# Experts sorted by token count on chip: four of eight in 64 slots with two products, weight splits in pairs, gates at the slots

## The reference

```python
logits = (t @ w_router).astype(jnp.float32)
top_vals, top_idx = lax.top_k(logits, TOP_K)
top_w = jax.nn.softmax(top_vals, axis=-1)
gates = jnp.sum(jax.nn.one_hot(top_idx, N_EXPERTS, dtype=jnp.float32) * top_w[..., None], axis=1)
out = jnp.zeros_like(t)
for e in range(N_EXPERTS):
    out = out + gates[:, e:e + 1].astype(t.dtype) * swiglu(t, w_gate[e], w_up[e], w_down[e])
```

## Time and profile before

| | |
|---|---|
| median of 3 runs | 1240.27 us |
| profiled execution, its own time | 1239.24 us |
| its span in the trace | 1237.4 us |
| mean granted TensorE clock | 0.993 of full |
| busy share: TensorE, weight loads, VectorE, ScalarE | 98%, 83%, 74%, 65% |
| bytes moved, mean rate | 294.48 MB, 238 GB/s |

### The profile page before, as it was taken

The page is one execution under the profiler, slowest core; times in us unless marked ns, Lnnn a source line. Parts: engine busy times, 40 slices in busy tenths (PEclk is TensorE's granted clock), DMA queues, the critical chain, the costliest instruction groups (busy, mean ns, idle before and its releaser), DMA issues.

```text
span 1237.4 us, 16333 instructions
## 1 busy us (share of the span) xinstructions
PE 1210.3 (98%) x5945; PEld 1029.4 (83%) x5945; DVE 920.6 (74%) x1157; ACT 802.2 (65%) x1035; POOL 17.9 (1%) x59
## 2 busy tenths in 40 slices
PE   8999999999999999999999999999999999999995
PEld 7887788888888888877888898888888888888884
DVE  5567666765545464686667699999989998999995
ACT  6555566454343455465564588888787888888882
POOL 2000000000000000000000000000000000000000
PEclk9999999999999999999999999999999999999997
DMA  9745423586555255554236489999999999999980
GB/s 325 231 144 184 137 93 111 181 294 231 185 177 196 94 162 199 162 170 162 90 111 203 169 306 382 331 347 352 338 341 332 358 340 344 332 354 347 362 306 36
DMA packets 119868, 294.48 MB, mean 238 GB/s; under 512 B 8958, under 2 KB 33628, under 8 KB 119276
## 3 DMA queue, kind: packets, MB, share of 16 engines
q1 hardware_dynamic: 118832, 288.66, 67.4%
q0 software_dynamic: 816, 4.75, 1.0%
q10 hardware_dynamic: 140, 0.04, 0.0%
HBM read 292.37 MB, written 1.05 MB: 237 GB/s over the span
## 4 chain that ended last, share of the span: by engine, by line
PE 90%; ACT 3%; DVE 3%; issue 2%; DMA 1%; SPq 0%; DVEq 0%; POOLq 0%; POOL 0%; ACTq 0%
PE bank L1316 27%; PE bank L1318 27%; PE bank L1317 27%; PE bank L1354 2%; DMA raw<-in_w_in 1%; PE bank L1638 1%; ACT w_hi L564 1%; PE bank L1661 1%; PE bank L1515 1%; PE bank L1495 1%; ACT p_buf L687 1%; DVE mixed L1065 1%; PE bank L1503 1%; PE bank L1487 1%; PE bank L1655 1%
## 5 line engine op out<-in xcount | busy, mean ns | idle before, releaser
L874 DVE TENSOR_TENSOR w_lo<-raw,w_hi 128x1536 fp32r<-128x1536 f32 (+3 forms) x144 | 242.9, 1693 | 178.6 <-ACT w_hi L564 178.0
L1316 PE MATMUL bank<-w_hi,aT_hi 128*128 128x512 f32 (+2 forms) x848 | 330.9, 390 | 3.4 <-DVE aT_lo L905 2.8
L1318 PE MATMUL bank<-w_hi,aT_lo 128*128 128x512 f32 (+2 forms) x848 | 324.3, 382 | 0.0
L1317 PE MATMUL bank<-w_lo,aT_hi 128*128 128x512 f32 (+2 forms) x848 | 324.0, 382 | 0.0
L1145 DVE SCALAR_TENSOR_TENSOR w_lo<-raw,cols,w_hi 128x896 fp32r<-128x896 f32 x256 | 287.7, 1150 | 32.7 <-ACT w_hi L740 29.0
L564 ACT ACTIVATE w_hi<-raw 128x1536 fp32r<-128x1536 f32 (+4 forms) x144 | 205.7, 1433 | 159.1 <-PE bank L1318 157.6
L740 ACT ACTIVATE w_hi<-raw,cols 128x896 fp32r<-128x896 f32 x256 | 265.5, 1045 | 64.9 <-PE bank L1318 61.6
L1316 PEld LDWEIGHTS bank<-w_hi,aT_hi 128*128 128x128 f32 x848 | 159.8, 188 | 29.9 <-DVE w_lo L970 2.1
L1318 PEld LDWEIGHTS bank<-w_hi,aT_lo 128*128 128x128 f32 x848 | 159.7, 188 | 26.7
L1317 PEld LDWEIGHTS bank<-w_lo,aT_hi 128*128 128x128 f32 x848 | 160.0, 189 | 24.5
L1316 PE MATMUL bank<-w_hi,bT_hi 128*128 128x448 f32 (+1 forms) x384 | 146.9, 382 | 0.7 <-issue 0.7
(11 more groups left out here) (230 smaller groups left out, 1119.6 us busy)
## 6 DMA issues: line engine op xcount, KB each, us to landing
raw<-in_moe_w_gate SPq DMA_DIRECT2D x128, 448.0 KB, 4.7
raw<-in_moe_w_up SPq DMA_DIRECT2D x128, 448.0 KB, 4.8
raw<-in_moe_w_down SPq DMA_DIRECT2D x112, 512.0 KB, 5.6
raw<-in_w_in SPq DMA_DIRECT2D x40, 768.0 KB, 4.5
raw<-in_dense_w_gate SPq DMA_DIRECT2D x22, 512.0 KB, 4.0
raw<-in_dense_w_up SPq DMA_DIRECT2D x22, 512.0 KB, 4.8
raw<-in_dense_w_down SPq DMA_DIRECT2D x11, 1024.0 KB, 4.9
raw<-in_w_in SPq DMA_DIRECT2D x20, 512.0 KB, 4.7
```

What stands on the lines that cost most here:

```text
L874: dve.tensor_tensor(w_lo[:, s, 0:n], raw[:, b % 2, j, 0:n], w_hi[:, s, 0:n].bitcast(F32), ALU.subtract).then_inc(lo_made[j], 1)
L1316: pe.matmul(dst, x_hi, b_hi, start=start, stop=False)
L1317: pe.matmul(dst, x_hi, b_lo, start=False, stop=False)
L1318: return pe.matmul(dst, x_lo, b_hi, start=False, stop=stop)
```

## The change

1. **Sorting.** The tokens per expert are counted as before; a key per expert (8 times the count, less its number; 4096 more for expert 0) is sorted by MAX, and `rank_of` reorders the slot numbers and gates by two multiplications and a reduction (`by_rank`). `order` holds the experts' numbers; SP reads one with `value_load` before each expert from the second on and loads its weights from the address it gives. Ranks 0 to 3 are the big experts of the four pairs, ranks 4 to 7 the small ones, as (big, small) pairs.
2. **64 slots, two products.** A small expert's stationary operand holds 64 tokens' high parts in its columns 0 to 63 and the low parts of the same tokens in 64 to 127; `small_product` multiplies both by w_hi and by w_lo. The low rows are then added to the high rows: ScalarE copies the bank (`fold_low`), TensorE adds it shifted by 64 rows (`add_folded`), once for the gate and once for the up product of a step. For the down product no folding is made: the rows of `sel` transposed stand twice, so `bring_back` adds both. The hidden of a small expert has 64 rows, is transposed in one go and evacuated by one instruction on each engine. A second round now also runs if the fifth key says more than 64 tokens.
3. **Paired splits.** Two neighbouring granules of one width in an even place are split by one instruction (`SPLITS`); raw slots and split slots come free by pairs.
4. **Gates at the slots.** `gates_to_slots` brings each slot's gate to its row, y_hi and y_lo are scaled by it (`slot_gate`), and one `bring_back` sums both experts of a pair, so `add_output` is a plain addition, 16 times instead of 32.
5. **Channel weights on the residual.** `weigh` makes hg = h * gain before routing; the splits have no scale. The gain buffer is loaded with `norm_ffn[1]`, then again with `norm_final` by the POOL queue.
6. `BETWEEN` is written anew for this.

```diff
+def is_small(k):
+    return k % 4 >= 2
+SPLITS = []
+for i in range(0, len(GRANULES), 2):
+    SPLITS += [(i, 2)] if granule_width(GRANULES[i][2]) == granule_width(GRANULES[i + 1][2]) else [(i, 1), (i + 1, 1)]
...
+BETWEEN = {(STEPS - 1, 22): ("hidden", STEPS - 1, 0)}
+for p in range(PAIRS_E):
+    k = 4 * p
+    BETWEEN[k, 11], BETWEEN[k, 13] = ("gate", p, 0), ("sel", p, 0)
+    for q, n in enumerate((3, 9)):
+        BETWEEN[k + 1, n], BETWEEN[k + 2, n] = ("hidden", k, q), ("hidden", k + 1, q)
+    BETWEEN[k + 3, 5] = ("hidden", k + 2, 0)
+    if p:
+        BETWEEN[k, 5] = ("hidden", k - 1, 0)
+        for q, n in enumerate((1, 5, 7, 11)):
+            BETWEEN[k + 2, n] = ("back", p - 1, q)
+    if p < PAIRS_E - 1:
+        for i, at in enumerate(((2, 13), (2, 15), (3, 1), (3, 3), (3, 7), (3, 9), (3, 11), (3, 13))):
+            BETWEEN[k + at[0], at[1]] = (("tokens_hi", "tokens_lo")[i // 4], p + 1, i % 4)
...
+                                    experts_at[k // 2] = sp.value_load(order[0:1, at_rank:at_rank + 1], min_val=0, max_val=EXPERTS - 1)
-                                sp.wait_ge(e_lo_made, RAW_BEFORE[i] + 1)
+                                sp.wait_ge(e_lo_made, SPLIT_OF[RAW_BEFORE[i]] + 1)
...
+                    if W_BEFORE[i] is None:
+                        act.wait_ge(used[i // 2], MIX[1] + BLK_MIX + 2)
+                    else:
+                        act.wait_ge(e_used, W_BEFORE[i + n - 1] + 1)
+                    act.activation(split_of(hi_slot, m), raw_of(i, n), ACT.Copy).then_inc(e_hi_made, 1)
...
+            def fold_low(r, k, banks, part):
+                s = small_steps(r, k)
+                act.wait_ge(e_used, SEQ[r, k, (KC, GU_N)[part] - 1] + 1)
+                if 2 * s + part:
+                    act.wait_ge(e_folded, 2 * s + part)
+                for u in range(2):
+                    act.activation(fold[:, u * HN:(u + 1) * HN], bank[banks[u]][:, 0:HN], ACT.Copy).then_inc(e_fold_made, 1)
...
+                def weigh(u):
+                    for t in range(NT):
+                        wait_read(dve, L, PAIR_MIX + u, t)
+                        part = slice(u * NB, (u + 1) * NB)
+                        dve.tensor_tensor(hg[:, t, part], h[:, t, part], gain[:, part], ALU.mult).then_inc(weighed, 1)
...
-                    dve.scalar_tensor_tensor(out=w_of(lo_slot, i), in0=raw_of(i), scalar=granule_scale(i),
-                                             in1=w_of(hi_slot, i).bitcast(F32), op0=ALU.mult, op1=ALU.subtract).then_inc(e_lo_made, 1)
+                    dve.tensor_tensor(split_of(lo_slot, m), raw_of(i, n), split_of(hi_slot, m).bitcast(F32),
+                                      ALU.subtract).then_inc(e_lo_made, 1)
...
+            def small_product(dst, x, b_hi, b_lo, start, stop):
+                pe.matmul(dst, x, b_hi, start=start, stop=False)
+                return pe.matmul(dst, x, b_lo, start=False, stop=stop)
+            def add_folded(r, k, banks, part):
+                s = small_steps(r, k)
+                for u in range(2):
+                    pe.wait_ge(e_fold_made, 4 * s + 2 * part + u + 1)
+                    last = pe.matmul(bank[banks[u]][:, 0:HN], shift[:, :], fold[:, u * HN:(u + 1) * HN], start=False, stop=True, skip_group_check=True)
+                last.then_inc(e_folded, 1)
```

382 lines of the change are left out of this document (250 added, 132 removed).

## The result

| | before | changed |
|---|---|---|
| median | 1239.53 us (4 runs) | 1211.74 us (4 runs, 1211.41 to 1212.18) |
| ratio, 95% interval | | 0.977 (0.976 to 0.978) |
| profiled execution | 1239.24 us | 1211.82 us |

What follows compares the result with a forecast made beforehand. TensorE was taken to bound the stage before, three engines nearly level after. Stage -29.7, ahead +1.7, behind +1.4 give -26.6 on 1239.24 us: 1212.6, forecast 1213 with the median 1 us higher; range 1192 to 1234.

Steps and rivals of the forecast that it cites:

- What is lost between them: Expert stage, ring of three slot pairs: slack 1.3 or 0.6 us, loss 1.2 us per step, 19 in all.
- Behind it: After the last splits: transpose and copies of the last hidden +1.5 us, bring-back -0.1; +1.4 in the sum.
- The TensorE term: Expert stage: two products instead of three for half the experts remove 78.7 us; TensorE then needs about 432 us.
- The VectorE and ScalarE terms: Expert stage: paired splits take 1.98 or 2.25 us on VectorE, about 1.65 or 1.86 on ScalarE.
- The largest of each: Four steps of an expert pair: largest engine need in each, together 115.1 us; times four, 460.4 us.
- Ahead of the stage: Routing: later copy, longer sorting chain +1.4 us, gathers giving back 0.9; first expert matmul +1.7 us.
- The loads and the register reads: Expert weight loads: address registers and seven register reads taken at nothing; up to 23 us without cover.
- B: Rival: transfers become the bound of the expert stage, at 346 GB/s; kernel 1231 us, chance 0.1.
- C: Rival, expert stage: ScalarE's extra instructions fall in full on VectorE's chain; stage 515 us, kernel 1249, chance 0.06.
- D: Rival: nothing is lost between the engines; stage 460.4 us, loads 377 GB/s, kernel 1194 us, chance 0.19.
- The signs: Trace marks of a right forecast: TensorE gaps ended by VectorE, VectorE over 90% busy, first expert matmul near 713.

Runs made afterwards that it cites:

- Experiment 9: Changed kernel with every granule split by its own instruction and a superfluous third product for the small experts: 1253.03 us.
- experiment 11: Changed kernel with every granule split by its own instruction and VectorE writing the low part of only half the columns: 1190.47 us.
- experiment 2: Changed kernel with every granule split by its own instruction and split slots freed one by one: 1191.51 us, 0.960 of the kernel before.
- experiment 1: Changed kernel with more spare matmuls keeping TensorE busy during routing: 1208.96 us, 0.975 of the kernel before.
- experiment 5: Changed kernel with the last hidden product one granule earlier and the first expert's last bring-back among the last down granules: 1213.67 us.
- experiment 4: Changed kernel loading only the first half of each expert weight granule's columns: 1210.3 us.
- 10: Changed kernel with the experts' order written in as constants instead of seven register reads: 1214.0 us, one run.
- experiment 8: Changed kernel with single splits, spare routing matmuls, channel multiplication behind the router's copy, and earlier last hidden with moved bring-back: 1188.74 us.

## Why the prediction came out right, point by point

**The total was right, and two errors in it cancel.** The stage with its end came 6 us better than the sum (-34.5 against -28.3 for "What is lost between them" and "Behind it" together). The time ahead of it came 5.5 us worse (+7.2 against +1.7); 3.0 of these were the clock in the routing, 1.4 the place of its fall at the program's start, and neither was in the prediction. That they nearly made up for the other error is luck. (The last step of the sum is rounded kindly, too: 1212.6 and the 1 us added are 1213.6, not 1213.)

**The TensorE term.** The removed 78.7 us are as counted. The need afterwards was too low: 109.3 us per four steps against 112.5 busy with single splits, 13 us in the stage (and the 432 us given for the whole stage don't agree with four times 109.3, which is 437). Experiment 9 gives 111.6 by another way, 131.3 less the 19.7 of the third product. Part is in sizes: four gather matmuls of 192 columns take 0.42 us, 0.106 each, and I had scaled their time with the columns. How the rest divides among transposes, folds and the switches between kinds of matmul, I didn't take apart.

**The VectorE and ScalarE terms** held. The listed durations of a pair are 2.02 and 2.29 us on VectorE, where the prediction worked out 2.024 and had 2.292 before it took off the overlap, and 1.71 and 1.92 on ScalarE. In four steps VectorE was busy 108.2 us against 110.0 forecast, ScalarE 96.0 against 98.2. The rule of 45 ns saved per instruction is seen as well: 2.0 us for 43 instructions fewer in four steps.

**"The largest of each" is the step that failed.** It gave 115.1 us for four steps, 5.8 above my TensorE need, because VectorE or ScalarE ruled both small steps. With single splits VectorE has more to do (110.2 us), the four steps still take only 113.8, and with VectorE's splits halved nothing changed (experiment 11). Two faults lie in it. The needs were dealt out to the wrong steps: counted from the first split of a step's granules to the first of the next step's, VectorE is busy 27.2 us in the small first half of the changed kernel, where the term put 30.2, and ScalarE 26.2 in the small second half, where it put 27.4. And surplus is carried over: in experiment 2 VectorE spends 27.4 busy us on the granules of the small second half, and TensorE gets through them in 26.0. That the slots between them and the mix of down and gate granules carry it is my reading; no run changes their number. The error of +5.8 was nearly undone by the TensorE need that was 3.2 too low.

**"What is lost between them" was right in size, 4.8 us per four steps against the 4.9 by which pairs are slower than singles, and I drew the wrong conclusion from it.** The prediction describes the ring: three pairs, 6.1 or 5.3 us to go round, 1.3 or 0.6 us of slack. The measured waits are its picture: longer ones (up to 1.9 us in the steady part, where singles and the kernel before have 0.6 and 0.7), three engines that each wait for the next. I had booked the paired instructions as a gain on VectorE first and the ring as a toll on it. Experiment 2 shows that without pairing there is neither and the kernel is 20 us faster: 17.4 in the steady stage (first to last silu 436.9 against 419.4), 1.3 before the first silu, 0.8 in the routing and 1.6 before it, of which 1.5 are the place of the clock's fall at the program's start, not the edit; behind the last silu 0.4 are lost again. The forecast should have asked whether the engine that pairing relieves was to be the bound at all.

**"Ahead of the stage": +1.7 forecast, +5.3 measured in the routing.** The parts named came as named: the last copy 0.45 + 1.3 later against 1.7 measured once the 1.9 us at the start are off, sorting +1.4 (1.58 instead of 0.20). The gathers, which were to give back 0.9 and take 2.9 us, take 3.7 at the full clock (experiment 1): 192 columns cost nearly what 256 did, 3.8. Missing is the clock: at 0.50 they take 6.3. Nothing in the earlier trace rows spoke of it, for they begin where the stage does; the windows between 700 and 712 had to be read. Of the other 1.9 us, before the router, 1.4 to 1.5 are not the change: kernels with the same code there start the router at 698.26 (experiment 5) and 699.75 (the changed kernel), by where the clock fell at the program's start. The remaining 0.4 I can't place.

**"Behind it": +1.4 forecast.** The serial piece that I had at +1.5 is there and larger: TensorE stands 4.1 us and loses 1.9 more at the lower clock, 6.0 us in all, which are inside the stage's 474.9. Behind the last expert matmul it is 16.7 us against 16.95.

**The loads and the register reads** at nothing: both right (experiments 4 and 10).

**The rivals.** B fell by experiment 4. C, the slower one, had the mechanism that exists: VectorE waited 43.4 us for ScalarE over the whole stage, under the 60 that I had set as its sign, and losses were 4.9 against the 11.4 where it decides. D, nothing lost between the engines, is what single splits give, at 1191.5, with the time I had for D (1194) nearly met, for TensorE's reasons and not for the ones given. The Trainium skill's limit of 358 GB/s (page "DMA: Bandwidth & Descriptors", Specifications) would have forbidden it; 389 GB/s over 380 us in experiment 2 settle that on one core it does not hold. The Trainium skill itself has the fitting sentence elsewhere: page "Perfetto Trace Analysis", Roofline, lets a single core that is alone exceed that share, up to about 120% of it. The trace of experiment 2 agrees, at 109%.

**The signs.** First expert matmul near 713: it was 718.5. Steps near 28, 31, 31.5, 28.5: 28.7, 33.4, 31.0, 25.2. Some of the second's 2.4 and the fourth's -3.3 is where the silu lies in a step, for a small expert's silu waits for its fold. VectorE over 90%: 91%. TensorE's gaps ended by VectorE: yes, 11.9 us of them at small experts' products and 1.6 at big ones between 740 and 1160; but the first of the four steps, a big one that begins with the small expert's down granules, has 1.5 us of them as well. ScalarE waiting for TensorE in big second halves only: no, in all four steps alike (4.4, 5.1, 3.1 and 4.3 us on L1459). I had written that a step in which an engine in second place is the one waited for makes the prediction wrong; by that sign its picture of the big steps is wrong, though the total stands.

## What to carry to other kernels

Merging two instructions of a buffer ring saves the fixed cost of one on its engine and halves the number of hand-overs that the ring can hold; here it lost, and it can pay only where that engine is the bound and the ring has room to spare, so count the time for one round of the longer pieces against the pace of the bound. To learn whether a 97% busy engine bounds anything, halve its work and look: here it was worth nothing in the steady stage and 1 us of 1190 in all. When work is moved to fill one wait, look at the place that it leaves: in experiment 8 the moved matmuls gained 1.3 us and cost 1.1. Take an execution apart by stages before a difference of 2 us is explained. When a chain of small instructions grows, look at TensorE's granted clock in its windows, and put spare matmuls in the gap.
